# The order of the experts: the sort key of experts with several blocks moved by one step

## The chip, the cores and the metric
The kernel runs on 1 core of one Trainium2 chip (trn2). The time is the device time of one execution in microseconds (us); lower is better. A profile of one execution stands beside it.

## What is computed
One step of a hybrid decoder layer for 512 prompt tokens and 8 sample tokens, in float32: a mixer (gated linear attention and sliding window attention), then a mixture of 32 experts of which each token uses 4, then a last norm. Only the experts matter here:

```python
logits = x2d @ w_router + b_router
top_v, top_e = lax.top_k(logits, TOP_K)            # 4 of 32 experts for each of 520 tokens
hh = xb @ w_up[e] + b_up[e]                        # (rows, 1024) @ (1024, 2048)
y  = clamped_swiglu(hh) @ w_down[e] + b_down[e]    # (rows, 1024) @ (1024, 1024)
```

The weights of one expert are 8 MiB (w_up) and 4 MiB (w_down). All 32 experts are read from HBM, some 400 MB. The result of a token is a sum over its experts, so the experts can be taken in any order.

## The kernel before
**Blocks.** The rows (token and slot) that chose an expert are cut into blocks of 64 rows (`SUB = 64`). An expert with 65 to 128 rows has two blocks, one with up to 64 rows has one. The blocks of an expert stand behind each other. Block b goes through two matrix products, `up(b)` and `down(b)`. The reference's router, worked out on its inputs, gives between 31 and 102 rows per expert; 14 experts have two blocks and 18 have one, 46 blocks in all (expert 0 counts as 80 rows, since its first block is made before its last tokens are known).

**Weights.** SBUF holds one expert's weights in 12 units of 1 MiB: 8 for `up`, 4 for `down` (`UPU, DNU = 8, 4`; the tile `raw`). SP issues the transfers. `load_up(e, j, cond)` and `load_down(e, j, cond)` (lines 598 to 614) carry a condition `is_new`: if the block belongs to the expert of the block before it, nothing is transferred, though the instruction and its wait stay. For each unit SP waits until TensorE has used it for the previous block:

```python
with sp.Fori(4, nb) as b:
    for j in range(UPU):
        sp.wait_ge(up_used, UPU * b + (j + 1 - UPU))   # up(b - 1) has used unit j
        load_up(e_up, j, new_up)
    load_downs(b)       # the w_down units of block b - 1, each as down(b - 2) has used it
```

So the transfers of a two-block expert's successor start as its second block uses the units. Ahead of the loop the same is written out for blocks 0 to 3; the first expert (0, two blocks) and the second (1, one block; half of its `up` units go to a buffer of their own, `ahead`) are fixed, and blocks 3 and later follow the table.

**TensorE.** In the loop: `up(b)`, `down(b - 1)`, `up(b + 1)`, `down(b)`, ... (lines 2159 and 2284), 64 and 32 instructions a block, each unit after its landing. GpSimd gathers the rows of a later block and scatters the results of an earlier one with indirect DMAs, one each per block; ScalarE and VectorE do bias, clamp, activation and the turns of the operands between.

**The end.** The w_down units of the last block have places of their own (`load_last_down`, line 747): they are loaded as `up` of the last block has used units 0 to 3. Then `load_slots` (line 760) reads the scattered results back, 8 transfers of 1 MiB, each into a unit that is free. VectorE weighs them (line 1756), adds the last two blocks' part, which TensorE makes from on-chip rows, and norms and stores (line 1744).

**The order.** VectorE makes a sort key for each expert in a row of 32. `rank_many` is the running count of experts with several blocks, `all_many` (M) their number. For s = 0, 1, ... the place of a one-block expert among the one-block ones, and r = 1, 2, ... that of a several-block expert among its own kind, the keys before are

- one block: (2s + 1)(M + 1)
- several blocks: (2r - 1)(33 - M) + 0.5

and experts 0 and 1 get -1 and -0.5. The experts are taken by rising key: both kinds are spread over the whole order.

Of the kernel before, what the change touches and what calls it, by code (L numbers as in the profile page):

```python
# [22 lines left out]
ALU = mybir.AluOpType  # L23
# [45 lines left out]
def moe_layer(nc, x_prompt, x_sample, state_gla, cache_k, cache_v, meta, bias_tab, g_mix, w_in, w_a_up, b_a,  # L69
# [11 lines left out]
    with ExitStack() as ctx:  # L81
# [218 lines left out]
        rank_many = B("rank_many", [P, NE])  # L300
        key = B("key", [P, NE])
        key_many = B("key_many", [P, NE])
# [102 lines left out]
        class Own:  # L405
# [5 lines left out]
            def step(self, ins):  # L411
                ins.then_inc(self.s, 1)
                self.n += 1
                return ins
# [4 lines left out]
            def do(self, ins):  # L419
                self.step(ins)  # L420
                self.settle()
# [662 lines left out]
        def _(dve):  # L1084
            own = Own(dve, dve_own)
            step, settle, do = own.step, own.settle, own.do
# [476 lines left out]
            step(dve.tensor_scalar(blk_count[:], blk_count[:], 1.0, None, ALU.add))  # L1563
            step(dve.tensor_scalar(weight[:, 0:1], all_many, -1.0, NE + 1.0, ALU.mult, ALU.add))
            step(dve.tensor_scalar(weight[:, 1:2], all_many, 1.0, None, ALU.add))
            do(dve.tensor_scalar(key_many[:], rank_many[:], 2.0, -1.0, ALU.mult, ALU.add))
            do(dve.scalar_tensor_tensor(key[:], slots_row[:, 0:NE], 2.0, key_many[:], ALU.mult, ALU.subtract))
            step(dve.tensor_scalar(key_many[:], key_many[:], weight[:, 0:1], 0.5, ALU.mult, ALU.add))
            do(dve.tensor_scalar(key[:], key[:], weight[:, 1:2], None, ALU.mult))
# [155 lines left out]
            step, do, settle = own.step, own.do, own.settle  # L1725
# [676 lines left out]
```

## Time and profile before

| | us |
|---|---|
| time, median of 3 runs (lowest, highest) | 1338.73 (1337.44, 1341.12) |
| the profiled execution: span of its instructions | 1337.8 |
| TensorE busy in the span | 1283.2 (96%) |
| VectorE busy in the span | 918.0 (69%) |
| issue by SP of the first w_up transfer in the loop over blocks | 374.41 |
| last instruction of VectorE begins | 1333.45 |

A busy TensorE is not one at its peak: ends of matmuls are modelled. The profiled execution's own time is its span and what lies around it; the span is 0.9 us under the median of the three runs. "Releaser" in a row is what ended a wait.

### The profile page before, as it was taken

How to read it: one execution, taken by the hardware profiler on the slowest of the kernel's cores; microseconds unless marked ns; L12 is line 12 of the kernel's file. 1: busy time of each engine (PE TensorE's matmuls, PEld its weight loads, DVE VectorE, ACT ScalarE, POOL GpSimd, SP SyncE). 2: the span in 40 equal slices, each digit the busy share in tenths (PEclk: the TensorE clock that was granted, in tenths of full speed). 3: DMA queues.
4: the chain of work that ended last, by engine and by line, in shares of the span. 5: the costliest groups of instructions: out<-in, count | busy, mean ns of one | idle time of the engine just before them, and what ended most of it. 6: DMA issues, size and time to landing. Idle time of an engine off the chain costs nothing.

```text
span 1337.8 us, 21359 instructions
## 1 busy us (share of the span) xinstructions
PE 1283.2 (96%) x6323; PEld 520.2 (39%) x6323; DVE 918.0 (69%) x1877; ACT 285.1 (21%) x542; POOL 124.1 (9%) x229
## 2 busy tenths in 40 slices
PE   8999999999999999997999998899999997999996
PEld 6876565553333333332333332233333331333332
DVE  3215357656878777775787786687777875777778
ACT  4331143433112121111121121111121111121114
POOL 2000000000020110100110101010111100110100
PEclk9998999999999999999999999999999999999999
DMA  9405154078999999999999999999999999999996
GB/s 358 129 4 191 32 176 170 32 284 342 417 386 386 421 421 419 416 421 421 420 398 423 414 422 420 414 422 407 420 417 420 414 421 421 421 402 420 412 414 274
DMA packets 91409, 468.95 MB, mean 351 GB/s; under 512 B 11870, under 2 KB 29520, under 8 KB 41074
## 3 DMA queue, kind: packets, MB, share of 16 engines
q1 hardware_dynamic: 75070, 441.56, 81.2%
q0 software_dynamic: 7360, 16.79, 3.2%
q10 hardware_dynamic: 8948, 10.19, 2.2%
q8 instruction: 19, 0.31, 0.1%
q14 instruction: 12, 0.10, 0.0%
HBM read 614.82 MB, written 28.77 MB: 481 GB/s over the span
## 4 chain that ended last, share of the span: by engine, by line
PE 71%; DMA 21%; DVE 4%; SPq 2%; issue 1%; ACT 0%; DVEq 0%; POOL 0%; POOLq 0%; ACTq 0%
PE ps L2159 34%; DMA raw<-in_w_down_dram 19%; PE ps L2284 17%; PE ps L1845 5%; PE ps L1822 5%; PE ps L2060 3%; SPq L614 1%; DMA raw<-slot_outputs 1%; PE ps L2173 1%; DVE v_gate L1756 1%; DMA x_rows<-expert_inputs,row_idx 1%; PE ps L1924 0%; PE ps L2007 0%; PE ps L2015 0%; PE ps L2014 0%
## 5 line engine op out<-in xcount | busy, mean ns | idle before, releaser
L2159 PE MATMUL ps<-raw,xT 128*64 128x512 f32 x2816 | 617.4, 593 | 17.6 <-DMA raw<-in_w_up_dram 17.0
L1632 DVE STREAM_TRANSPOSE xT<-x_hold 32x192 f32<-32x192 f32 (+2 forms) x680 | 275.0, 404 | 154.1 <-PE ps L2159 133.9
L2159 PEld LDWEIGHTS ps<-raw,xT 128*64 128x64 f32 x2816 | 199.9, 137 | 424.6 <-issue 391.0
L2284 PE MATMUL ps<-raw,aT 128*64 128x512 f32 x1408 | 317.1, 595 | 16.7 <-DMA raw<-in_w_down_dram 16.7
L1632 DVE STREAM_TRANSPOSE aT<-act_g 32x256 f32<-32x256 f32 x352 | 223.5, 635 | 64.4 <-PE ps L2284 54.5
L2284 PEld LDWEIGHTS ps<-raw,aT 128*64 128x64 f32 x1408 | 97.6, 137 | 229.2 <-issue 174.7
L1016 ACT ACTIVATE act_s<-act_g 128x512 f32<-128x512 f32 x46 | 29.0, 630 | 632.6 <-DVE act_g L1616 632.6
L566 POOL DMA_INDIRECT slot_outputs<-y_rows,out_idx x44 | 45.2, 1028 | 609.3 <-ACT y_rows L1021 608.4
L1404 DVE STREAM_TRANSPOSE bias_up<-up_cols 128x1024 f32<-128x1024 f32 x46 | 57.3, 1245 | 1.6
L1845 PE MATMUL ps<-w_c_cols,hT 128*128 128x512 f32 x128 | 56.8, 596 | 0.0
L558 POOL DMA_INDIRECT x_rows<-expert_inputs,row_idx x47 | 49.3, 1049 | 71.2 <-issue 53.5
L1021 ACT ACTIVATE y_rows<-ps 128x512 f32<-128x512 f32 x45 | 26.9, 597 | 99.0 <-PE ps L2284 99.0
L2060 PE MATMUL ps<-w_out_sb,mixT 128*128 128x512 f32 x96 | 42.8, 599 | 0.1
L1012 ACT ACTIVATE x_hold<-x_rows 128x512 f32<-128x512 f32 x45 | 28.3, 630 | 59.6 <-DVE xT L1632 58.5
L1616 DVE TENSOR_SCALAR act_g<-ps 128x512 f32<-128x512 f32 x46 | 31.8, 692 | 10.8 <-PE ps L2159 9.5
L1822 PE MATMUL ps<-hT,w_a_cols 128*128 128x268 f32 x160 | 36.6, 390 | 0.0
L1845 PEld LDWEIGHTS ps<-w_c_cols,hT 128*128 128x128 f32 x128 | 23.7, 190 | 27.8 <-issue 27.8
L1623 DVE TENSOR_TENSOR act_g<-act_l,act_s 128x512 f32<-128x512 f32 x46 | 31.8, 692 | 1.6
L1621 DVE SCALAR_TENSOR_TENSOR act_l<-act_l,act_g 128x512 f32<-128x512 f32 x46 | 31.8, 692 | 1.4
L966 ACT ACTIVATE ps<-bias_up 128x512 f32<-128x512 f32 x47 | 28.3, 601 | 20.8 <-DVE bias_up L1404 13.8
L1822 PEld LDWEIGHTS ps<-hT,w_a_cols 128*128 128x128 f32 x160 | 30.3, 190 | 6.1 <-issue 0.4
L1617 DVE TENSOR_SCALAR act_l<-ps 128x512 f32<-128x512 f32 x46 | 31.3, 681 | 0.0
(405 smaller groups left out, 899.7 us busy)
## 6 DMA issues: line engine op xcount, KB each, us to landing
raw<-in_w_up_dram SPq DMA_DIRECT2D x356, 1024.0 KB
raw<-in_w_down_dram SPq DMA_DIRECT2D x180, 1024.0 KB, 10.5
slot_outputs<-zeros ACTq DMA_DIRECT2D x1, 8320.0 KB, 27.9
ahead<-in_w_up_dram SPq DMA_DIRECT2D x8, 1024.0 KB
raw<-slot_outputs SPq DMA_DIRECT2D x8, 1024.0 KB, 16.1
w_c_cols<-in_w_in_dram SPq DMA_DIRECT2D x1, 4096.0 KB, 31.1
w_out_sb<-in_w_out_dram SPq DMA_DIRECT2D x1, 4096.0 KB, 13.8
w_a_cols<-in_w_in_dram SPq DMA_DIRECT2D x1, 2624.0 KB, 12.3
```

The lines of the kernel that those rows point to most:

```text
L558: pool.indirect_dma_start(x_rows[:], None, xn_halves, bass.IndirectOffsetOnAxis(ap=idx[:, 0:1], axis=0), bounds_check=last_row, oob_is_err ...
L566: pool.indirect_dma_start(slot_halves, bass.IndirectOffsetOnAxis(ap=out_idx[:, 0:1], axis=0), y_rows[:], None, bounds_check=last_out, oob_ ...
L1404: return dve.transpose(bias_up[:].rearrange("p a (c r) -> p (a c) r", r=32), bc(up_cols[:], 2, [P, 2 * COLS, 32]))
L1616: dve.tensor_scalar(act_g[:], ps[:, banks[0], :], LIMIT, None, ALU.min).then_inc(g_ready, 1)
L1621: o.do(dve.scalar_tensor_tensor(act_l[:], act_l[:], 1.0, act_g[:], ALU.add, ALU.mult))
L1623: dve.tensor_tensor(act_g[:], act_l[:], act_s[:], ALU.mult).then_inc(a_ready, 1)
L1632: dve.transpose(dst_at(rows_out, group), src_at(rows_in, parity)).then_inc(done, 1)
L1822: ins = mm(ps[:, n % 4, 0:HALF], w[:, k, c0:c0 + P], hT[:, k, half], start=(k == 0), stop=(k == KT - 1))
L1845: ins = mm(ps[:, bank, 0:n], hT[:, k, a:z], w[:, k, c0:c0 + n], start=(k == 0), stop=(k == KT - 1))
L2060: ins = mm(ps[0:r, 6 + n, :], mixT[:, k, 0:r], w_out_sb[:, k, 512 * n:512 * n + 512], start=(k == 0), stop=(k == KT - 1))
L2159: ins = mm(ps[SUB * i:SUB * i + SUB, banks[bank], :], rows_in[:, j, :], weights[:, c:c + HF], start=False, stop=(j == at_end), skip_group_ ...
L2284: ins = mm(ps[SUB * i:SUB * i + SUB, 2, :], aT[:, j, r, :], raw[:, units[j], D * r + HF * i:D * r + HF * i + HF], start=False, stop=(j == ...
```

## The change
One constant in the sort key: `key_many` is 2 * rank - 2 where it was 2 * rank - 1. No instruction is added or removed. The keys become

- one block: (2s + 2)(M + 1)
- several blocks: (2r - 2)(33 - M) + 0.5

With the counts above the order of the experts (blocks of each, in order; a pair "21" is a two-block expert and a one-block one) is

```
before: 21 1 21 21 21 1 21 21 21 1 21 21 21 21 1 21 21 21
after:  21 21 21 21 1 21 21 21 21 1 21 21 21 21 1 21 21 1
experts before: 0 1 3 2 5 4 6 8 7 9 11 10 12 16 13 17 18 14 21 15 22 19 23 20 25 27 24 28 26 29 30 31
experts after:  0 1 2 3 4 5 8 6 7 11 9 12 10 13 16 14 17 18 15 21 19 22 20 23 24 25 27 26 28 30 29 31
```

```diff
             step(dve.tensor_scalar(weight[:, 0:1], all_many, -1.0, NE + 1.0, ALU.mult, ALU.add))
             step(dve.tensor_scalar(weight[:, 1:2], all_many, 1.0, None, ALU.add))
-            do(dve.tensor_scalar(key_many[:], rank_many[:], 2.0, -1.0, ALU.mult, ALU.add))
+            do(dve.tensor_scalar(key_many[:], rank_many[:], 2.0, -2.0, ALU.mult, ALU.add))
             do(dve.scalar_tensor_tensor(key[:], slots_row[:, 0:NE], 2.0, key_many[:], ALU.mult, ALU.subtract))
             step(dve.tensor_scalar(key_many[:], key_many[:], weight[:, 0:1], 0.5, ALU.mult, ALU.add))
             do(dve.tensor_scalar(key[:], key[:], weight[:, 1:2], None, ALU.mult))
```

## Rows read from the trace of the kernel before

**Rows 1.** The page: the span in 40 equal slices, and the costliest groups and issues.

```profile
PE   8999999999999999997999998899999997999996
...
DMA  9405154078999999999999999999999999999996
GB/s 358 129 4 191 32 176 170 32 284 342 417 386 386 421 421 419 416 421 421 420 398 423 414 422 420 414 422 407 420 417 420 414 421 421 421 402 420 412 414 274
...
L1016 ACT ACTIVATE act_s<-act_g 128x512 f32<-128x512 f32 x46 | 29.0, 630 | 632.6 <-DVE act_g L1616 632.6
...
raw<-in_w_up_dram SPq DMA_DIRECT2D x356, 1024.0 KB
```

**Rows 2.** The chain of waits in order of time: start us, us, what.

```profile
384.92 6.87 PE ps L2284 x32
391.79 13.73 PE ps L2159 x64
...
446.72 6.89 PE ps L2284 x32
453.93 19.93 DMA raw<-in_w_down_dram
...
517.39 19.67 DMA raw<-in_w_down_dram
...
603.77 27.57 DMA raw<-in_w_down_dram
...
1241.09 19.73 DMA raw<-in_w_down_dram
...
1298.88 16.49 DMA raw<-slot_outputs
```

**Rows 3.** The timeline of SP's queue: start us, us, line, operation, tile, count.

```profile
387.36 5.10 SPq L614 DMA_DIRECT2D raw<-in_w_down_dram  x4
394.79 11.14 SPq L604 DMA_DIRECT2D raw<-in_w_up_dram  x8
407.71 5.36 SPq L614 DMA_DIRECT2D raw<-in_w_down_dram  x4
415.35 11.44 SPq L604 DMA_DIRECT2D raw<-in_w_up_dram  x8
428.56 4.85 SPq L614 DMA_DIRECT2D raw<-in_w_down_dram  x4
435.75 11.64 SPq L604 DMA_DIRECT2D raw<-in_w_up_dram  x8
449.15 5.11 SPq L614 DMA_DIRECT2D raw<-in_w_down_dram  x4
...
1285.49 5.28 SPq L747 DMA_DIRECT2D raw<-in_w_down_dram  x4
...
1292.87 11.48 SPq L760 DMA_DIRECT2D raw<-slot_outputs  x8
```

**Rows 4.** Windows: length, busy PE, PEld, DVE, ACT, POOL, granted clock, DMA share, GB/s.

```profile
374.00:376.00 2.00, 2.00 (x12) 0.72 (x10) 1.75 (x3) 1.38 (x3) 0.40 (x1) 1.00 0.43 92
384.00:386.00 2.00, 2.00 (x12) 0.61 (x10) 1.88 (x5) 0.00 (x0) 0.00 (x0) 1.00 1.03 434
406.00:408.00 2.00, 2.00 (x12) 0.65 (x10) 1.94 (x4) 0.71 (x2) 0.00 (x0) 1.00 0.59 246
408.00:410.00 2.00, 2.00 (x12) 0.65 (x10) 1.81 (x7) 1.04 (x2) 0.00 (x0) 1.00 0.64 164
610.00:620.00 10.00, 6.85 (x30) 1.93 (x32) 1.49 (x3) 0.00 (x0) 0.18 (x1) 1.00 1.02 422
```

**Rows 5.** The timeline of the end of the span, all engines.

```profile
1305.59 7.09 PE L2284 MATMUL ps<-raw,aT_last 128*64 128x512 f32 x32 [0.35 <-ACT ps L1007]
...
1319.43 3.93 DVE L1756 SCALAR_TENSOR_TENSOR v_gate<-raw,gates,v_gate 128x1024 f32<-128x1024 f32 x3
...
1333.45 1.28 DVE L1744 SCALAR_TENSOR_TENSOR v_gate<-v_gate,t_stat,g_final_bc 128x1024 f32<-128x1024 f32 x1
```

## The prediction

> **What bounds the kernel.** I read the page first. Its slices say two things at once [rows 1]: TensorE is busy in tenths of 9 and more nearly everywhere, and from the fourteenth slice on the DMA engines are too, at 400 to 423 GB/s. Both can't be the bound, and a busy TensorE proves little, since its ends are modelled. The chain of waits in order of time decides it [rows 2]. Up to 453.6 us it is TensorE alone, 13.73 us for an `up` and 6.87 us for a `down`, 20.6 us a block: here the transfers are ahead and wait for units. From 453.93 on the chain goes every 63 to 94 us through a transfer of w_down, on which TensorE waits: from there the stream of weights is the bound. The windows bear that out: between 610 and 620 us TensorE is busy 6.85 of 10 us while the DMA share is full at 422 GB/s, and the clock stays at 1.00 of its rate, the 2.4 GHz level [rows 4].
>
> So there are two phases. In the first, a hole in the stream appears whenever SP must wait for TensorE: 246 and 164 GB/s in the windows at 406 and 408 us, 92 at 374 [rows 4]. Nobody makes good what a hole loses, because the second phase runs at the stream's rate to the end. The changed order must be judged by these holes, not by TensorE's share.
>
> **Prices of the second phase.** The ends of the DMA pieces in the chain are moments at which the last w_down unit of a one-block expert lands and TensorE has caught up with the stream: 473.86, 537.06, 631.34, and at the end 1260.82 [rows 2]. Between the first two lies a pair "21" (24 units, 3 blocks): 63.20 us. Between the next two lie a pair and a single more: 94.28 us. A single one-block expert thus costs 31.1 us, where TensorE alone would need 20.6; the pair costs 63.2 where TensorE needs 61.8. Check: from 473.86 to 1260.82 the order before has 11 pairs and 3 singles, 11 x 63.20 + 3 x 31.1 = 788.5 against 787.0 in the rows, 0.2% off. The 46 blocks agree with the 46 sigmoids [rows 1]; that rules out that expert 3, with exactly 64 rows, became a two-block one.
>
> **The change, part by part.** *The instruction.* One constant of a VectorE operation on 32 elements; nothing is added, cost 0 with or without cover. SP, GpSimd and ScalarE execute the same instructions, the same 384 MiB of weights are moved, each row is gathered and scattered as before. Only which SP transfers are skipped by their condition, and when, changes.
>
> *The start.* Blocks 0 to 2 are the same experts. Before, block 3 is expert 3 (one block) and blocks 4 and 5 are expert 2; after, blocks 3 and 4 are expert 2 and block 5 is expert 3. So block 4 is now a second block: the 8 `up` units that SP issued from 374.41 us on are not transferred, though SP still waits for each. The next real transfers are w_down of block 3, which SP issues from 387.36 us, when `down(2)` at 384.92 frees the places, and then `up` of block 5 from 394.79 [rows 3], where before it skipped 8. In the window at 374 us the stream had already run dry (92 GB/s [rows 4]), so from then to about 388 it stays empty: some 14 us, against holes of 3.6 us in the order before in the three windows shown (421 GB/s less what each moved, over 2 us: 1.6, 0.8 and 1.2).
>
> When does the stream catch TensorE again? Before, the same figure stands one block later: 4 w_down issued at 407.71 after a skip, 8 `up` at 415.35, 8 at 435.75, 4 w_down at 449.15, and the last lands at 473.86: 66.15 us from the first issue. After, the same 24 units go out at 387.36, 394.79, 415.35 and 428.56 [rows 3], the same distances within 0.3 us, since SP's waits there follow TensorE's fixed pace. I take the same 66.15 us: the w_down of expert 3 lands at 453.5. TensorE begins that `down` at 446.72 [rows 2] and is caught inside it. The second phase begins 20.35 us earlier than before, one block of TensorE's pace.
>
> *The rest.* From there before had 11 pairs, 3 singles, and expert 30 with expert 31 as the last pair: 12 pairs, 3 singles. After has 12 pairs (4 with 5, 8 with 6, ... 30 with 29), 3 singles in the middle (7, 18, 27), and expert 31 as a fourth: one single more, 31.1 us. The shift of the stream is 31.1 - 20.35 = +10.75 us. In words: the one-block expert that stood third was loaded while TensorE was behind, so it cost only TensorE's 20.6 us; now it stands last and costs the stream's 31.1.
>
> *The end.* Before, expert 31 follows a two-block one. TensorE is behind there: the last product starts at 1305.59 and takes 7.09 us [rows 5], and the w_down transfers it needs landed at about 1302.8 (the fifth slot read lands at 1315.37 [rows 2], less five MiB at 2.49 us, which is 1.049 MB at 421 GB/s); it ends 9.8 us behind them. After, it ends about 1.7 us behind its last landing, the time of a quarter of the 6.87 us, so 8 us sooner against the stream. That gain I count at 0: behind the last weights the stream carries 8 MiB of slot reads, issued from 1292.87, ahead of need [rows 3], and VectorE works on them as they land; its last part runs until 1333.45 and then stores [rows 5]. In the new order the places are free in time too: `up` of the last block follows the landing of its units, and 4 of w_down of block 44 and 4 of block 45 still lie between that and the first slot read. If the cover were gone, 8 us would be to be had.
>
> *Small.* The block before the last isn't scattered; it now holds expert 29's 58 rows instead of 7 of expert 30: 51 rows of 4 KB less, 0.5 us at 420 GB/s. Sum: +10.75 - 0.5 = +10.3 us; the span goes from 1337.8 to 1348.1, the time from the median 1338.7 to 1349.0.
>
> **Bounds.** The refill of 66.15 us may be 2 us off either way, as the gathers fall. The one pair that stands alone in the rows took 63.20, the mean of eleven is 63.06; over 12 of them that is 1.7 us, and I allow twice that. The likeliest case by itself: 1346 to 1352.5.
>
> **A rule beside the row.** The stream's rate decides whether a hole can be made good. The rows show 421 GB/s as the level of the loop and 434 as the best short window [rows 1, 4]. The Trainium skill, "DMA: Bandwidth & Descriptors", section "Where 436 GB/s comes from", puts the limit at 435.2 GB/s, with the ports as the bottleneck. By that figure the 328 units left would take 2.41 us each where the row gives 2.49, some 26 us less, and no loss would be left. No slice of this trace runs above 423, whatever waits behind it, so the sum goes by the row.
>
> **The rivals.** *The stream makes the hole good.* After the hole it would have to run at 426 GB/s instead of 421 (10.3 us over 328 units of 2.49 us); single windows do [rows 4], but behind the hole at 406 the slices show the level and not more [rows 1]. Time 1338.7; chance 0.04.
>
> *TensorE bounds, so the end pays (faster).* If the 96% of TensorE were real and the holes in the stream free, only the end would count: the last product done 8 us sooner, 1330.6. It decides from the point at which the transfers wait for TensorE in most of the loop, slices well under 420 GB/s. For it: TensorE's row; against it: the window at 610. Chance 0.05.
>
> *Less loss.* The 8 us at the end free part of the last stretch: from the last weighing at 1323.4 to the last norm at 1333.45 lie 10.1 us [rows 5]. If a third of that (an estimate) is waiting for TensorE's and ScalarE's work on the last blocks, 3.3 us go and 1345.7 is left. Chance 0.09.
>
> *More loss.* Four pairs in a row at the start, where before had one and then three: if each of 12 pairs costs 0.3 us more (twice that difference) and the refill 2 us more, +16: 1354.5. Chance 0.10.
>
> *No change of order.* The keys are all different, so another constant must move experts; it would take other counts than worked out. 1338.7, chance 0.02.
>
> **The numbers.** My case has 0.70. Beyond 0.3% (4 us) a measurement of this kernel tells a change from none. Slower: 0.70 + 0.09 + 0.10 = 0.89; same: 0.06; faster: 0.05. The range of 8 in 10 takes my case and most of both neighbours: 1345 to 1354. Predicted 1349.0.
>
> **What the profile after would show.** The slice at 370 to 390 us falls from about 400 GB/s to near half. In the chain TensorE is alone only to about 447, and the first DMA piece ends near 453.5; then come ends near 517 and 611, with the same distances of 63 and 94 us, and one catch at about 1304 that wasn't there before. SP issues 8 real transfers at 394.79. The last product of `aT_last` is broken by waits for its weights. The prediction is wrong if the stream shows no hole at 375 to 388, if the first catch comes much later than 453.5, or if slot reads begin later behind the last weights than now.

## The result and the profile after

The changed kernel takes 1349.49 us (median; 1348.33 to 1351.62), against 1338.73 before: ratio 1.0076, interval 1.0062 to 1.0091. It is slower by 10.8 us; 10.3 were forecast. The profiled execution has a span of 1347.1 us, 9.3 more than the one of before; its early part happens to be 1.08 us ahead (the `up` that began at 391.79 [rows 2] begins at 390.71), which makes 10.4.

The page after: the slices of TensorE, of the DMA engines and their GB/s, then the bytes of the queue that gathers and scatters.

```profile
PE   8999999999999999979999999889999999799995
...
DMA  9505164088969999999999999999999999999996
GB/s 355 128 4 190 32 201 143 32 325 334 414 229 421 421 421 412 421 421 421 408 414 411 421 411 422 421 421 421 405 420 415 420 420 421 421 418 398 422 414 270
...
q0 software_dynamic: 7360, 16.59, 3.2%
```

One slice stands out against [rows 1]: the twelfth, 229 GB/s where it had 386. All others of the loop are at the level of before. The last line had 16.79 MB before: the 0.2 MB of scatters that were expected to fall away.

The windows of 20 us from 370 us on, where the hole was expected; first the kernel before, then the changed one (columns as in rows 4).

```profile
370.00:390.00 20.00, 20.00 (x96) 6.71 (x94) 17.67 (x35) 4.25 (x8) 3.53 (x6) 1.00 0.92 365
390.00:410.00 20.00, 20.00 (x96) 6.65 (x94) 15.75 (x31) 3.42 (x6) 2.45 (x4) 1.00 0.94 377
410.00:430.00 20.00, 20.00 (x96) 6.75 (x94) 15.73 (x31) 3.58 (x6) 2.45 (x4) 1.00 1.01 406
430.00:450.00 20.00, 20.00 (x96) 6.62 (x94) 15.73 (x31) 3.33 (x6) 2.45 (x4) 1.00 1.02 421
450.00:470.00 20.00, 20.00 (x96) 6.65 (x94) 15.75 (x31) 2.98 (x6) 2.46 (x4) 1.00 1.01 420
```

```profile
370.00:390.00 20.00, 20.00 (x96) 6.70 (x94) 18.71 (x36) 4.72 (x8) 2.96 (x5) 1.00 0.33 109
390.00:410.00 20.00, 20.00 (x96) 6.75 (x94) 15.72 (x32) 3.57 (x6) 2.46 (x4) 1.00 1.01 405
410.00:430.00 20.00, 20.00 (x96) 6.61 (x93) 15.69 (x33) 2.97 (x7) 2.46 (x4) 1.00 1.01 421
430.00:450.00 20.00, 19.43 (x92) 6.22 (x90) 15.75 (x31) 3.55 (x6) 2.46 (x4) 1.00 1.01 420
450.00:470.00 20.00, 19.45 (x90) 6.30 (x92) 14.12 (x26) 2.07 (x4) 2.46 (x4) 1.00 1.02 422
```

In the first two windows TensorE is busy 20 of 20 us in both kernels. Only the stream tells them apart: 109 for 365 GB/s, then 405 for 377. Over the five windows the changed kernel moved what 10.1 us of stream at 421 GB/s carry less than the kernel before.

SP's queue and the chain of waits after:

```profile
386.03 5.36 SPq L614 DMA_DIRECT2D raw<-in_w_down_dram  x4
393.73 11.39 SPq L604 DMA_DIRECT2D raw<-in_w_up_dram  x8
```

```profile
390.71 13.73 PE ps L2159 x64
...
432.26 20.06 DMA raw<-in_w_down_dram
...
495.84 19.43 DMA raw<-in_w_down_dram
...
582.94 26.96 DMA raw<-in_w_down_dram
...
1219.61 19.22 DMA raw<-in_w_down_dram
...
1297.50 27.18 DMA raw<-slot_outputs
```

The first catch is at 452.32, where the kernel before had 473.86 [rows 2]. From there the chain repeats that of before with the same distances: 63.0, then 94.6, and 786.5 us from the first catch to 1238.83, the one ahead of the last pair, where before had 787.0 (11 pairs and 3 singles in both).

The end after (timeline, all engines):

```profile
1301.29 1.94 PE L2284 MATMUL ps<-raw,aT 128*64 128x512 f32 x8 [0.40 <-DMA raw<-in_w_down_dram]
...
1308.74 1.94 PE L2284 MATMUL ps<-raw,aT_last 128*64 128x512 f32 x8 [0.27 <-DMA raw<-in_w_down_dram]
1311.71 1.94 PE L2284 MATMUL ps<-raw,aT_last 128*64 128x512 f32 x8 [1.03 <-DMA raw<-in_w_down_dram]
...
1342.75 1.28 DVE L1744 SCALAR_TENSOR_TENSOR v_gate<-v_gate,t_stat,g_final_bc 128x1024 f32<-128x1024 f32 x1
```

The last product now runs piece by piece behind its weights, where before it ran unbroken from 1305.59 [rows 5]. From the landing of the fifth slot read to the end of the span it is 22.4 us in both (1315.37 to 1337.8 before, 1324.68 to 1347.1 after).

### The profile page after: what moved, and what is told of

Read it like the earlier page. It is cut to its first block, busy times and chain, and to the rows that moved or that the text cites. A ratio compares the mean times of both kernels' runs of the same rounds, so it can differ in the third digit from the quotient of the medians.

```text
span 1347.1 us, 21359 instructions
## 1 busy us (share of the span) xinstructions
PE 1286.3 (95%) x6323; PEld 520.2 (39%) x6323; DVE 918.1 (68%) x1877; ACT 285.0 (21%) x542; POOL 124.9 (9%) x229
## 4 chain that ended last, share of the span: by engine, by line
PE 69%; DMA 25%; DVE 3%; SPq 1%; issue 1%; ACT 0%; DVEq 0%; POOL 0%; POOLq 0%; ACTq 0%
PE ps L2159 32%; DMA raw<-in_w_down_dram 22%; PE ps L2284 17%; PE ps L1822 5%; PE ps L1845 5%; PE ps L2060 3%; DMA raw<-slot_outputs 2%; SPq L614 1%; PE ps L2173 1%; DVE v_gate L1756 1%; DMA x_rows<-expert_inputs,row_idx 1%; DMA x_sb<-in_x_prompt_dram 0%; PE ps L1924 0%; PE ps L2007 0%; PE ps L2015 0%
## 5 line engine op out<-in xcount | busy, mean ns | idle before, releaser
L2284 PE MATMUL ps<-raw,aT 128*64 128x512 f32 x1408 | 317.5, 595 | 16.7 <-DMA raw<-in_w_down_dram 16.6
L2284 PEld LDWEIGHTS ps<-raw,aT 128*64 128x64 f32 x1408 | 97.5, 137 | 229.7 <-issue 173.8
L1616 DVE TENSOR_SCALAR act_g<-ps 128x512 f32<-128x512 f32 x46 | 31.8, 691 | 10.7 <-PE ps L2159 9.5
L1617 DVE TENSOR_SCALAR act_l<-ps 128x512 f32<-128x512 f32 x46 | 31.3, 680 | 0.0
```

The lines of the kernel that those rows point to most:

```text
L1616: dve.tensor_scalar(act_g[:], ps[:, banks[0], :], LIMIT, None, ALU.min).then_inc(g_ready, 1)
L2284: ins = mm(ps[SUB * i:SUB * i + SUB, 2, :], aT[:, j, r, :], raw[:, units[j], D * r + HF * i:D * r + HF * i + HF], start=False, stop=(j == ...
```

## The experiments

All orders were made by giving single experts another key behind the line that sets the key of expert 1. That is one or two more VectorE operations, ahead of everything that is measured here; the lines behind it move by one or two, so L2285 in these kernels is L2284 of the kernel before. "Before" is the kernel before on the same chip, 1338.4 to 1338.5 us in all three sets.

**The start of the change with the end of before** (on the changed kernel):

```diff
             step(dve.memset(key[:, 1:2], -0.5))
+            step(dve.memset(key[:, 31:32], 150.25))
```

> The changed kernel with expert 31 taken from the last place to the tenth (21 21 21 21 1 1 21 ...): the start is that of the change, the end is that of before (a two-block and a one-block expert last). My theory (only the empty stretch of the stream at the start costs, the end is worth nothing): 10.3 to 11 us over before, 1349 to 1350, as the changed kernel; the last two blocks scatter as before, so 0.5 us more than the changed one. Rival (the end with two one-block experts is worth up to 8 us to the changed kernel): then this one loses them and takes 1356 to 1358. The first catch by a w_down transfer stays near 453, the last product of aT_last runs unbroken again.

Measured: 1349.59 us, ratio 1.0077 (1.0063 to 1.0091). The whole loss is there without the end. The first catch in this kernel's chain is at 454.9. The last product, in the timeline of this kernel, is in one piece again:

```profile
1317.40 7.09 PE L2285 MATMUL ps<-raw,aT_last 128*64 128x512 f32 x32 [0.34 <-ACT ps L1007]
```

**The end of the change with the start of before** (on the kernel before):

```diff
             step(dve.memset(key[:, 1:2], -0.5))
+            step(dve.memset(key[:, 9:10], 600.0))
```

> The kernel before with expert 9 taken from the tenth place to the last: start 21 1 21 as before, end 21 1 as in the change. My theory: the end is hidden behind the slot reads, so 1338.2 (0.5 us of scatters less), within 0.2% of before. Rival (the end pays up to 8 us): 1330.6 to 1332. Second rival (a one-block expert in last place costs by itself, whatever stands at the start): 1343 or more.

Measured: 1338.48 us, ratio 0.9999 (0.9989 to 1.0009). The end alone is worth nothing that can be told from noise (the interval is some 1.3 us to either side), though TensorE finishes the last product earlier: in this kernel's timeline its last piece begins at 1301.73 and takes 1.94 us, where before ended at 1312.7 [rows 5].

```profile
1298.45 1.94 PE L2285 MATMUL ps<-raw,aT_last 128*64 128x512 f32 x8 [0.30 <-DMA raw<-in_w_down_dram]
1301.73 1.94 PE L2285 MATMUL ps<-raw,aT_last 128*64 128x512 f32 x8 [1.35 <-DMA raw<-in_w_down_dram]
```

Nine us sooner on TensorE (1.1 of them because this execution's first catch, at 472.74 for 473.86, was already that much earlier), and nothing of it arrives. This also refutes that a one-block expert in last place by itself costs the 4 us or more of the second rival.

**One step against the change: two one-block experts behind the second** (on the kernel before):

```diff
             step(dve.memset(key[:, 1:2], -0.5))
+            step(dve.memset(key[:, 9:10], 50.0))
```

> The kernel before with expert 9 in the fourth place: 21 1 1 21 ... . A step further in the direction opposite to the change. The theory of the holes: block 5 is then a new expert, the 8 w_up transfers that SP issues at 394.8 are real ones and the hole at 406 to 410 goes; that hole is worth 2 to 3 us, so 1335.5 to 1337; the first catch comes at about 436 to 441 instead of 473.9. Rival (each one-block expert moved to the start saves the 10.7 us that the change loses): 1328.

Measured: 1336.22 us, ratio 0.9983 (0.9974 to 0.9992). The window of this kernel from 390 us on, and its first catch in the chain:

```profile
390.00:410.00 20.00, 20.00 (x96) 6.71 (x94) 15.72 (x32) 3.29 (x6) 2.45 (x4) 1.00 1.01 418
```

```profile
411.94 27.25 DMA raw<-in_w_down_dram
```

The hole at 406 [rows 4] is closed, 418 GB/s for 377, and TensorE is caught at 439.2. The gain is about that of the hole, 2.3 us, and not another 10.7.

**Three of them** (on the kernel before, keys 50.0 and 51.0 for experts 9 and 18):

> The kernel before with experts 9 and 18 in the fourth and fifth place: 21 1 1 1 21 ... . Theory: with two one-block experts behind the third place the last hole that the order can close is closed, TensorE is caught at block 4; one more has nothing left to close: as with 21 1 1, 1335.5 to 1337. Rival (each such move gives back about 2 us): 1334.

Measured: 1336.45 us, ratio 0.9979 (0.9970 to 0.9988): as with two. One more closes nothing further; the window at 370 to 390 still moves 358 GB/s.

**Two two-block experts behind each other in the middle** (on the kernel before):

```diff
             step(dve.memset(key[:, 1:2], -0.5))
+            step(dve.memset(key[:, 13:14], 215.0))
```

> The kernel before with expert 13 moved one place ahead: ... 21 2 2 1 1 1 ... in the middle of the order, start and end untouched. Theory: two two-block experts behind each other make TensorE late by more than the 12 units can bridge, the stream has a hole of about 8 us there, and all of it stays: 1345 to 1347. Rival (only the start is sensitive; in the middle the lead is made good by the one-block experts that follow): 1338.7.

Measured: 1346.44 us, ratio 1.0058 (1.0045 to 1.0072), 8.0 us slower. The windows of this kernel show the hole:

```profile
710.00:720.00 10.00, 10.00 (x50) 3.42 (x48) 8.83 (x20) 2.54 (x5) 2.27 (x3) 1.00 1.01 422
720.00:730.00 10.00, 10.00 (x50) 3.33 (x48) 6.92 (x12) 0.48 (x1) 0.18 (x1) 1.00 0.19 76
730.00:740.00 10.00, 10.00 (x48) 3.30 (x46) 8.83 (x19) 3.09 (x6) 2.27 (x3) 1.00 0.90 332
```

Against 421 GB/s the second and the third of these windows lack 8.2 and 2.1 us, 10.3 in all; 8.0 of it are in the time. The rest is no riddle: the stream of the kernel before isn't at 421 all the time in this stretch either. First its windows of 100 us, then those of this kernel:

```profile
660.00:760.00 100.00, 98.37 (x456) 32.05 (x454) 76.14 (x151) 17.19 (x29) 10.00 (x17) 1.00 1.01 412
760.00:860.00 100.00, 91.57 (x415) 28.43 (x413) 70.96 (x139) 15.01 (x26) 12.09 (x19) 1.00 1.01 418
```

```profile
660.00:760.00 100.00, 99.46 (x464) 33.01 (x462) 78.76 (x156) 17.89 (x30) 12.10 (x19) 1.00 0.92 373
760.00:860.00 100.00, 83.80 (x366) 23.99 (x364) 60.94 (x122) 13.49 (x23) 7.55 (x13) 1.00 1.01 421
```

That is 8.6 us of stream less than before over the 200 us. Three one-block experts come right after the hole, and none of them makes it good. So the start isn't special; it is only the place where the change puts a second block that TensorE isn't ready for.

**Two two-block experts more at the start** (on the kernel before, keys 10.0 and 20.0 for experts 2 and 4):

> The kernel before with experts 2 and 4 in third and fourth place: 21 2 2 1 1 1 21 ... . Theory: one more block of TensorE's pace in the first phase, in which the stream waits; the holes add up: 18 to 20 us over before, 1357 to 1359 (twice the change's loss, less the hole that before had). Rival (the loss of the change is a single restart and doesn't grow): 1349.

Measured: 1357.76 us, ratio 1.0145 (1.0127 to 1.0164), 19.3 us slower. This kernel has the change's hole at 370 to 390, and a second at 410 to 430:

```profile
370.00:390.00 20.00, 20.00 (x96) 6.64 (x94) 18.42 (x36) 4.73 (x8) 2.65 (x5) 1.00 0.31 109
390.00:410.00 20.00, 20.00 (x96) 6.72 (x94) 16.14 (x32) 3.58 (x6) 2.45 (x4) 1.00 1.01 409
410.00:430.00 20.00, 20.00 (x96) 6.73 (x94) 15.72 (x32) 3.55 (x6) 2.45 (x4) 1.00 0.60 239
430.00:450.00 20.00, 20.00 (x96) 6.63 (x94) 15.69 (x33) 2.99 (x7) 2.45 (x4) 1.00 1.01 405
450.00:470.00 20.00, 20.00 (x96) 6.75 (x94) 15.75 (x31) 3.57 (x6) 2.45 (x4) 1.00 1.01 421
```

The holes add up: over the five windows the stream lacks 19.3 us at 421 GB/s against the kernel before, and 19.3 us are in the time.

**TensorE's work cut, in both kernels.** In `down`, for all blocks from 3 on but the last, half of the matmuls are left out:

```diff
-                    for r in range(2):
+                    for r in ((0, 1) if at_last or isinstance(b, int) else (1,)):
                         for i in range(2):
                             ins = mm(ps[SUB * i:SUB * i + SUB, 2, :], aT[:, j, r, :],
```

(The expectation below names block 2 too; `down(2)` has a constant for b and stays whole, as do those of blocks 0 and 1.)

> The kernel before, whose down products in and next to the loop (block 2 and all from the loop over blocks on, but the last) leave out half of their matmuls (the first of the two rows of weights in each unit), so that a block costs TensorE 17.2 instead of 20.6 us; the output lacks these products. Theory (the stream bounds the loop): within 2 us of before, 1337 to 1340, though some 140 us of TensorE's work are gone. Rival (TensorE bounds): 60 to 140 us faster.

> The same cut in the changed kernel, again without half of the down products in the loop. Theory: the hole at the start depends on when SP may refill (up(4) and down(2), which keep their time or nearly so), not on TensorE's share: 9 to 11 us over the cut kernel before. Rival: with TensorE 17% faster per block the hole and the loss go, no difference between the two cut kernels.

Measured: 1338.38 us for the cut kernel before, ratio 0.9998 (0.9988 to 1.0009), and 1349.21 for the cut changed kernel, ratio 1.0078 (1.0061 to 1.0095), both against the uncut kernel before. The group of `down` in the cut kernel before:

```profile
L2284 PE MATMUL ps<-raw,aT 128*64 128x512 f32 x736 | 196.6, 659 | 63.6 <-DMA raw<-in_w_down_dram 63.6
```

736 matmuls for 1408: some 144 us of TensorE's work are gone (672 at the 0.215 us that 32 in 6.87 us give), and the time doesn't move. TensorE's busy time fell by less, from 1283.2 to 1191.6 us: the matmuls that are left take longer on average (659 ns for 595 in this group), some of them at a lower granted clock (last section). The loss of the change stays at 10.8 us, and so does its hole: 102 GB/s at 370 to 390 in the cut changed kernel, 365 in the cut kernel before. One detail was off: where the weights were ahead, a block took TensorE 18.8 us instead of 17.2, because it waited up to 1.5 us for VectorE's turn of `xT` (26 such waits in the span, 35.1 us); the timeline of the cut kernel before:

```profile
494.50 13.95 PE L2159 MATMUL ps<-raw,xT 128*64 128x512 f32 x64 [1.46 <-DVE xT L1632]
508.28 3.60 PE L2284 MATMUL ps<-raw,aT 128*64 128x512 f32 x16
513.33 10.52 PE L2159 MATMUL ps<-raw,xT 128*64 128x512 f32 x48 [1.45 <-DVE xT L1632]
```

## Why the prediction was right

**The bound.** Two phases, TensorE first and then the stream of weights. For the second the cut kernels show it: some 144 us of work less on TensorE change nothing. They don't test the first, since all that TensorE does ahead of the hole is uncut. That TensorE's pace sets the hole is read from the rows (busy 20 of 20 us, while SP's issues follow it), and fits the two holes with experts 2 and 4 in third and fourth place; no run made TensorE faster there.

**The hole.** Forecast: empty from about 374 to 388. In windows of 2 us the changed kernel moved 0 to 131 GB/s from 374 to 386, 115 at 386 and 410 at 388. From 370 to 390 it moved 109 for 365 GB/s, which is 12.2 us of stream at 421 GB/s less than before; of before's later hole 1.3 us come back at 390 to 410 (405 for 377) and 0.7 at 410 to 430 (421 for 406). The net is 10.1, near the loss of 10.8. The slice was forecast to fall to near half, and fell to under a third: 14 empty us of 20, the prediction's own figure, already give that.

**The first catch.** 66.15 us after SP's issue at 387.36 were forecast. It came 66.29 us after the issue at 386.03. The refill was read from the same figure one block later in the trace of before, and that reading held.

**The rest.** One single more, 31.1 us, was forecast. The pair at the end, 62.4 us (1238.83 to about 1301.2, the wait ahead of the piece at 1301.29), and 23.5 from there to the fifth slot read make 85.9, against 54.6 in the kernel before from 1260.82: 31.3. With the catch 20.5 us earlier (21.54, less the 1.08 by which this execution was ahead) and 0.5 us less in between, the sum is 10.3. The extra catch forecast near 1304 is no piece of the chain; in the timeline it is the wait that ends at 1301.29.

**The end at 0.** Shown by both exchanges: the end alone 0.9999, the start alone all of the loss. TensorE is 8 to 9 us sooner there and the slot reads hide it. SP issues the first slot read 7.3 us behind the first w_down of the last block (7.4 before). The eight issues then take 16.4 us instead of 11.5 [rows 3]; why is open, but the stream stays at 397 to 424 GB/s in every window of 5 us from 1300 to 1325, so it costs nothing that shows.

**The rivals.** A stream that makes its hole good: refuted three times, by the change, by the hole in the middle and by the two at the start; the page's slices never rise over 423 GB/s behind a hole. (The prediction counts 328 units behind the catch; its own order has 28 experts there, 336 units. The rate that this rival asks for stays 426 GB/s.) The limit of 435.2 GB/s that the Trainium skill gives ("DMA: Bandwidth & Descriptors", "Where 436 GB/s comes from") is not reached in any slice of these runs' pages; the level here is 421, and the best window of 2 us shown has 434 [rows 4]. TensorE as the bound of the loop: refuted by the cut. Less loss through the last stretch: 22.4 us in both, refuted. More loss through four pairs in a row: the stretch of 11 pairs and 3 singles took 786.5 for 787.0, refuted. No change of order: the 8 `up` units that SP goes through from 373 us on aren't transferred any more, as the 109 GB/s show, refuted.

## What to carry to other kernels

When two resources take nearly the same total time, find for each stage which one waits, and price a change of order by the emptiness that it makes in the stream that bounds the rest; a one-block expert that is loaded while TensorE is behind costs only TensorE's pace (20.6 us here), and the same expert later costs the stream's (31.1). Put the pieces that need the stream most and the engine least where the engine is late: two one-block experts behind the second, instead of one, is the best order found, 1336.2 us (with three it is the same within the noise). A gain at the end counts only for what isn't hidden behind the last transfers.

## What was not expected of the hardware

In the cut kernel the granted clock of TensorE fell, where the kernel before kept 1.00 through a window with 6.85 of 10 us busy [rows 4]. Windows of the cut kernel before:

```profile
466.00:470.00 4.00, 2.04 (x8) 0.28 (x8) 3.69 (x12) 2.38 (x4) 0.00 (x0) 1.00 1.02 426
470.00:474.00 4.00, 1.74 (x6) 0.49 (x8) 0.65 (x1) 0.00 (x0) 0.00 (x0) 0.86 1.00 418
474.00:478.00 4.00, 4.00 (x16) 1.27 (x14) 2.52 (x4) 1.20 (x2) 1.23 (x2) 0.71 1.02 424
```

In the windows at 466 and 470 us TensorE was busy 2.04 and 1.74 of 4 us, waiting for weights. In windows of 1 us the grant is 1.00 up to 472, 0.94 in the next, 0.50 (the 1.2 GHz level) from 473 to 476, and 1.00 (the 2.4 GHz level) again at 477. The mean over the span was 0.961, for 0.995 in the kernel before. The time didn't move with it (1338.38 us), and the stream stayed at 418 to 426 GB/s in these windows; a price of the lower clock doesn't show here, since TensorE wasn't what the loop waited for.
